# Joining the high and low half of the input in one 512-column product, in the five transposed projections of the first mixer

## What is computed

```python
h = rmsnorm(x, mix_pre_g)
u, v_s, q, k, v_a, g_a, g_b, f_logit = jnp.split(h @ w_in, IN_SPLITS, axis=-1)   # seven of width 1024
y_a = spatial_gating(gelu(u), gelu(v_s), w_spatial, b_spatial, sgu_norm_g)      # u * (W v + b) in chunks of 128
y_b = forgetting_attention(q, k, v_a, f_logit, b_forget)                        # 8 heads of 128
merged = sigmoid(g_a) * y_a + sigmoid(g_b) * y_b
x = x + rmsnorm(merged @ w_out, mix_post_g)
x = x + rmsnorm((silu(h2 @ w_gate) * (h2 @ w_up)) @ w_down, ffn_post_g)         # h2 = rmsnorm(x, ffn_pre_g), width 2816
```

## Time and profile before

| | |
|---|---|
| median of 3 runs | 1494.17 us (1492.42 to 1496.42) |
| the profiled execution's own time | 1493.1 us |
| its span, first to last instruction | 1491.4 us |
| what lies around the span | 1.7 us |
| PE busy / DVE busy / ACT busy | 1149.6 / 459.9 / 394.9 us |
| mean granted TensorE clock | 0.878 of 2.4 GHz |

### The profile page before, as it was taken

How to read it: one execution, slowest core, us unless ns; L and a number is a source line. 1 busy time by engine, 2 the same in 40 slices (tenths; PEclk the granted TensorE clock), 3 DMA queues, 4 the chain that set the end, 5 groups by cost and what they waited for, 6 DMA issues and landing times.

```text
span 1491.4 us, 19642 instructions
## 1 busy us (share of the span) xinstructions
PE 1149.6 (77%) x8524; PEld 758.9 (51%) x8524; DVE 459.9 (31%) x923; ACT 394.9 (26%) x880; POOL 69.7 (5%) x83
## 2 busy tenths in 40 slices
PE   9999999999997997897566566565665565565677
PEld 8998988888876875442223223223222232232234
DVE  6555777656778854010000000000000000000002
ACT  5655567555655644100000000000000000000002
POOL 0000020000033411000000000000000000000000
PEclk9999999999999999898778787777777787887789
DMA  8435546555553388999999999999999999999996
GB/s 308 175 123 217 182 185 218 205 211 200 195 187 115 113 337 358 381 437 437 428 440 428 432 435 430 432 436 429 435 426 442 428 435 430 431 433 432 428 423 286
DMA packets 29163, 503.33 MB, mean 337 GB/s; under 512 B 4115, under 2 KB 4755, under 8 KB 8085
## 3 DMA queue, kind: packets, MB, share of 16 engines
q1 hardware_dynamic: 25200, 493.43, 79.5%
q10 hardware_dynamic: 3876, 8.65, 1.7%
HBM read 501.02 MB, written 1.05 MB: 337 GB/s over the span
## 4 chain that ended last, share of the span: by engine, by line
issue 63%; PE 31%; DVE 2%; ACT 2%; POOL 1%; DMA 1%; ACTq 0%; POOLq 0%; DVEq 0%
PE PB L99 30%; PE PB L102 1%; DMA AG<-in_ag_dram 1%; DVE SPL L108 1%; ACT SPH L105 1%; POOL SPL L108 0%; DVE XN L116 0%; DMA RAW<-in_wst_dram 0%; POOL SM L136 0%; POOL SP L112 0%; DVE AQK L108 0%; ACT XN L105 0%; ACTq L156 0%; DVE SM L128 0%; ACT SP L105 0%
## 5 line engine op out<-in xcount | busy, mean ns | idle before, releaser
L99 PE MATMUL PB<-RING,XS 128*32 128x512 f32 x2048 | 292.7, 720 | 175.9 <-DMA RING<-in_wgu_dram 172.2
L99 PE MATMUL PB<-XT,SPH 128*128 128x256 f32 (+1 forms) x1056 | 252.3, 321 | 0.0
L99 PEld LDWEIGHTS PB<-RING,XS 128*32 128x32 f32 x2048 | 67.5, 126 | 346.6 <-DMA RING<-in_wgu_dram 187.6
L99 PE MATMUL PB<-RING,HHT 128*32 128x256 f32 x2048 | 151.7, 454 | 110.4 <-DMA RING<-in_wdn_dram 108.8
L108 DVE TENSOR_TENSOR SPL<-RAW,SPH 128x512 fp32r<-128x512 f32 x316 | 209.0, 720 | 40.6 <-ACT SPH L105 38.4
L99 PE MATMUL PB<-XT,SPL 128*128 128x256 f32 x704 | 201.0, 285 | 0.0
L105 ACT ACTIVATE SPH<-RAW 128x512 fp32r<-128x512 f32 x340 | 187.0, 621 | 9.4 <-DMA RAW<-in_wst_dram 5.2
L99 PEld LDWEIGHTS PB<-XT,SPH 128*128 128x128 f32 x1056 | 175.8, 190 | 16.7
L99 PEld LDWEIGHTS PB<-RING,HHT 128*32 128x32 f32 x2048 | 71.5, 130 | 175.3 <-DMA RING<-in_wdn_dram 112.7
L105 ACT ACTIVATE SG<-PB 128x512 f32<-128x512 f32 (+1 forms) x21 | 11.9, 566 | 509.1 <-PE PB L99 507.7
L99 PEld LDWEIGHTS PB<-XT,SPL 128*128 128x128 f32 x704 | 133.9, 190 | 0.5
(11 more groups left out here) (309 smaller groups left out, 1254.4 us busy)
## 6 DMA issues: line engine op xcount, KB each, us to landing
RAW<-in_wst_dram SPq DMA_DIRECT2D x84, 1024.0 KB, 4.8
RING<-in_wgu_dram SPq DMA_DIRECT2D x13, 2048.0 KB, 40.3
RING<-in_wgu_dram SPq DMA_DIRECT2D x14, 1024.0 KB, 8.4
RING<-in_wdn_dram SPq DMA_DIRECT2D x6, 2048.0 KB, 12.3
RING<-in_wgu_dram SPq DMA_DIRECT2D x2, 4096.0 KB, 19.6
RING<-in_wdn_dram SPq DMA_DIRECT2D x2, 4096.0 KB, 18.2
RING<-in_wdn_dram SPq DMA_DIRECT2D x3, 1024.0 KB, 41.8
RAW<-in_wst_dram SPq DMA_DIRECT2D x4, 256.0 KB, 5.8
```

The lines of the kernel that those rows point to most:

```text
L99: return pe.do(lambda e: e.matmul(out_, lhsT, rhs, start=start, stop=stop), after)
```

## The change

`XT`, the transposed input, is laid out anew: the high and the low half stand side by side for each feature block (`[P, KD, 2, T]` in place of `[P, 2, KD, T]`), so that the 512 columns are one run. `wide` replaces `wblock_ffn`, and takes the place of `wblock` in the five projections. `joined` adds the two halves of the bank: ACT copies the upper half into the destination, DVE adds the lower half to it (with the scale of q). In g_b, g_a and u the tanh or gelu then runs on the destination in SBUF.

```diff
-    XT = place("XT", [P, 2, KD, T], F32R, at(15))
-    XTH, XTL = XT[:, 0, :, :], XT[:, 1, :, :]
+    XT = place("XT", [P, KD, 2, T], F32R, at(15))
+    XTH, XTL = XT[:, :, 0, :], XT[:, :, 1, :]
...
+    def wide(u, s, bank):
+        hi, lo, got = unit(u)
+        hv = hi[:, :].rearrange("p (k c) -> p k c", k=KD)
+        lv = lo[:, :].rearrange("p (k c) -> p k c", k=KD)
+        for k in range(KD):
+            after = [got[k // 2], *xt] + (held[bank] if k == 0 else [])
+            mm(PB[bank][:, :], hv[:, k, s * P:(s + 1) * P], XT[:, k, :, :].rearrange("p w t -> p (w t)"), k == 0, False, *after)
+            t = mm(PB[bank][:, 0:T], lv[:, k, s * P:(s + 1) * P], XTH[:, k, :], False, k == KD - 1)
+        if s == 1:
+            unit_free[u] = t
+        bg(2)
+        return t
+
+    def joined(dst, bank, w, *after, scale=1.0):
+        a = act(dst, PB[bank][:, T:512], ACT.Copy, w, *after, scale=scale)
+        d = stt(dst, PB[bank][:, 0:T], scale, dst, ALU.mult, ALU.add, a)
+        held[bank] = [d]
+        return d
...
-        w = wblock(u + b // 2, b % 2, bk, XTH, XTL, xt)
-        gu[b] = act(GU[b % 3][:, :], PB[bk][:, 0:T], ACT.Gelu_apprx_tanh, w, gu_free.get(b - 3))
-        held[bk] = [gu[b]]
+        w = wide(u + b // 2, b % 2, bk)
+        gu[b] = act(GU[b % 3][:, :], GU[b % 3][:, :], ACT.Gelu_apprx_tanh, joined(GU[b % 3][:, :], bk, w, gu_free.get(b - 3)))
...
-        w0 = wblock_ffn(uu, 0, b0)
-        w1 = wblock_ffn(uu, 1, b1)
+        w0 = wide(uu, 0, b0)
+        w1 = wide(uu, 1, b1)
```

More of the change, by code:

```diff
@@ L659, in build @@
             bk = bank()
-            w = wblock(u + b // 2, b % 2, bk, XTH, XTL, xt)
+            w = wide(u + b // 2, b % 2, bk)
             dst = QT if b < 4 else KT
-            a = act(dst[:, h, :], PB[bk][:, 0:T], ACT.Copy, w, scale=P ** -0.5 if b < 4 else 1.0)
-            held[bk] = [a]
+            a = joined(dst[:, h, :], bk, w, scale=P ** -0.5 if b < 4 else 1.0)
             (q_ok if b < 4 else k_ok)[h] = a
@@ L676, in build @@
         bk = bank()
-        w = wblock(u + b // 2, b % 2, bk, XTH, XTL, xt)
-        tgb[b] = act(TGB[:, b, :], PB[bk][:, 0:T], ACT.Tanh, w, scale=0.5)
-        held[bk] = [tgb[b]]
+        w = wide(u + b // 2, b % 2, bk)
+        tgb[b] = act(TGB[:, b, :], TGB[:, b, :], ACT.Tanh, joined(TGB[:, b, :], bk, w), scale=0.5)
         fox_slot(4 + b, 4, 8)
@@ L728, in build @@
         bk = bank()
-        w = wblock(u + b // 2, b % 2, bk, XTH, XTL, xt)
-        tga[b] = act(TGA[:, b, :], PB[bk][:, 0:T], ACT.Tanh, w, scale=0.5)
-        held[bk] = [tga[b]]
+        w = wide(u + b // 2, b % 2, bk)
+        tga[b] = act(TGA[:, b, :], TGA[:, b, :], ACT.Tanh, joined(TGA[:, b, :], bk, w), scale=0.5)
         if b >= LAG:
@@ L830, in ffn_up @@
         hid["lo", f] = tt(HTL[:, f % 8, :], FT[2 + f % 2][:, :], HTH[:, f % 8, :].bitcast(F32), ALU.subtract, h, hfree.get(f - 8))
[L832 to L844, removed]
     def ffn_down(f, uu, kk, tile, nf):
```

## The result

| | before | changed |
|---|---|---|
| median of 12 runs | 1493.62 us (eleven from 1491.98 to 1496.42, one of 5936.88) | 1496.57 us (1495.40 to 1498.27) |
| ratio | 1 | 1.0021, 95% interval 1.0014 to 1.0029 |
| the profiled execution's own time / its span | 1493.1 / 1491.4 us | 1495.4 / 1493.6 us |
| mean granted TensorE clock | 0.878 | 0.873 |

The time lies in the range given (1488.8 to 1498.0), but the forecast was 1.6 us faster, and the kernel is 3.1 us slower (0.0021 x 1493.6).

A forecast was written before the change was run, and what follows sets the result against it. TensorE was taken to set the pace in the first mixer, with DVE nearly full in u, and expert-weight DMA the end. -2.6 - 2.4 + 3.4 = -1.6 us gave a median of 1492.6 us, range 1488.8 to 1498.

The forecast's parts named there:

- The layout for the feed-forward: Feed-forward up-projections: with the 512 columns contiguous, 352 pairs go from 0.3533 to 0.3467 us, -2.4 us (bounds -2.4 and 0).
- rival A: Joined pairs in projections and feed-forward stay at 0.3533 us, whatever the halves' distance: +2.1 us, 1496.3 us; chance 0.20.
- 24 x 8 x 0.0133 = -2.6: The 24 blocks of q, k and g_b: fewer products save 0.0133 us in each of eight groups, -2.6 us.
- Hidden, 0 us: Added evacuation in q, k and g_b: one DVE add of 0.42 us a block, covered by idle DVE and banks, 0 us.
- u's loop of 3.51 us: In u, one turn between ACT and DVE takes 3.51 us a block, against 2.77 for TensorE's block.
- forecast 3.35: Transposes after u: bank 1 free at 198.7 instead of 195.35 us, as TensorE waits for DVE's last add; +3.4 us.
- g_a's loop: In g_a, each block is a loop between ACT and DVE of 2.6 us; u's first add stands at 174.0 us.
- Rivals B: In u, the ACT and DVE loop keeps up and TensorE finds its banks: -5.5 us, 1488.7 us; chance 0.15.
- D: In u, the ACT and DVE loop takes 4.0 us rather than 3.51: +1.9 us alone, 1496.1 us; chance 0.10.
- Rival C, the clock: After TensorE's waits ahead of the output projection, the clock falls to 1.2 GHz: +2, total +0.4 us, 1494.6 us; chance 0.10.
- I count a microsecond won or lost before 440 us as one at the end: Expert weights' loads set the end and begin when earlier compute frees buffers, so earlier gains or losses carry over one for one.

The follow-up runs named there:

- k9_entry: The changed kernel with ten kinds of products, in turn, ahead of each half of the five feed-forward groups; one execution, 1499.3 us.
- k1_layout: The kernel before with only the new layout of XT and the feed-forward's contiguous pair, the five projections in their old form; 1493.33 us, ratio 0.9997.
- k11_u_alone: The kernel before with u alone in the new form and XT's new layout; 1499.61 us, ratio 1.0041.
- k5_phase: The kernel before with one plain fp32 product of 128 columns ahead of each of the five feed-forward groups; 1496.55 us, ratio 1.0020.
- k7_busy_less: The changed kernel with 8 and 11 plain fp32 products of the identity in TensorE's two pauses ahead of the memory transposes; 1496.43 us, ratio 1.0020.
- k2_u_old: The changed kernel with u alone in its old form (three products, gelu straight from PSUM); 1493.3 us, ratio 1.0001.
- k8_u_old_again: The changed kernel with u alone in its old form, run a second time; 1493.62 us, ratio 0.9999.
- k10_order: The changed kernel with MTH and MTL of the block before ahead of u's gelu, and the memory's transposes split; 1494.29 us, ratio 1.0005.

## Why the prediction was wrong

- **"The layout for the feed-forward: 352 pairs go from 0.3533 to 0.3467, -2.4 us."** This is the step that failed. The two distances were there, but I took the layout for their cause because it was the only difference I saw between the earlier trace rows. What came ahead of the stream differed too, and k9_entry shows both distances with the same operands. Measured 0 (k1_layout). That was rival A, at 0.20; without this term the sum already was on the other side of zero, at +0.8. The second step is the clock, which the sum had at 0 and which cost 1.5 in the trace (below).
- **"24 x 8 x 0.0133 = -2.6"** for q, k and g_b: measured -1.9 at the last v_s product. The first q and k blocks run at 0.353, those between the attention's steps gain 0.10 a block.
- **"Hidden, 0 us"** for the adds of q, k and g_b: right. TensorE is busy 53.95 of 54 us, and its blocks there became shorter.
- **u's loop of 3.51 us:** right, 3.55, with every part within 0.05 us of what was worked out (DVE idle 0.79, forecast 0.8). Against the end of v_s, the transposes into bank 1 start 3.85 us later than before, forecast 3.35: 0.3 by where the loop starts (g_a's loop takes 2.63, forecast 2.6, eight times), 0.2 by the loop itself. Rivals B (a loop that keeps up) and D (4.0 us) are out.
- **Rival C, the clock:** it came true as well, at 1.5 us of the 2 it gave: 1.2 in the transposes and 0.3 between the first two products of the output projection. I had given 0.10 to a case that two pauses of 2.20 and 2.83 us, with 0.63 of work between them, brought about. The Trainium skill ("TensorE: Matmul & The Clock Gate", part 1) has the clock fall after idle time; the rows agree, with a granted clock of 0.50 from 196 to 198 us. I had treated A and C as exclusive, and both happened.

From -1.6: +2.4 (layout) +0.7 (q, k, g_b) +0.5 (wait) +1.5 (clock) = +3.5 us. The trace has +3.4 at the feed-forward, the runs +3.1.

"I count a microsecond won or lost before 440 us as one at the end" held for this kernel and for k11_u_alone (+6.0 in the trace, 1.0041 measured), but not for every loss: k5_phase has +1.1 in the trace and +3.0 in the time, k7_busy_less +2.2 and +3.0. So the good agreement of +3.4 and +3.1 owes something to luck; what bears the sum is the trace up to the feed-forward. Leads of 1.7 to 1.9 us at the first expert product were not seen at the end in k2_u_old, k8_u_old_again and k10_order.

## What to carry to other kernels

Before a bank's evacuation is given to two engines, write out one turn of the loop that this closes between them, and look at what each has in its list between the two handovers: here one instruction placed behind the wait (`MTH` behind the gelu) made the loop 3.55 us instead of 2.91, and cost the 3.1 us by which this kernel is slower. A small difference between two spacings of the same product is not owed to the operands until the same operands have been seen at both. And where TensorE is let wait near the end of a part, price the clock after the pause with the pause.

## What the hardware showed that was not expected

- The same pair of products has two steady distances, 0.3467 and 0.353 us; what stands ahead can pick one, and it held over 48 pairs and more.
- The clock's return at the first expert products does not follow from when TensorE gets there: 596.61 us and back within 598 to 600 before, 594.80 and 595.27 and back within 602 to 604 with u in its old form, 594.75 and back within 598 to 600 in k10_order.
- Twelve transposes took 1.29 us at 2.4 GHz and 2.48 at 1.2, after 2.83 us of pause; with one pause of 1.92 us the clock stayed at 2.4.
